# In-projection and gated recurrence as one program: heads' projections between the recurrence's tiles

## The chip, the cores and the metric

The kernel runs on one core of a Trainium2 chip. The metric is the device time of one execution in microseconds (us). TensorE (PE) multiplies, VectorE (DVE), ScalarE (ACT) and GpSimd (POOL) work elementwise, and SyncE (SP) issues most transfers. Each engine takes its instructions in program order; semaphores order the engines among each other.

## What is computed

Two layers over 1152 tokens: 1024 of a new stream (the prompt) and 8 running streams of 16 tokens (the sample). The change concerns the mixer of the first layer, from `hn = rmsnorm(x)`:

```python
z = hn @ w_in                                   # q, k: 4 heads x 128; v, g: 4 x 256; a: 16
la = log_sigmoid(a @ w_gate2 + b_gate) / 16     # per token, head and key channel
b  = cumsum(la)                                 # inside blocks of 64 (sample: 16) tokens
qd, kd = q * exp(b), k * exp(-b)
A  = tril(qd @ kd.T)
o  = qd @ s + A @ v                             # s: state of the head, 128 x 256
s  = s * exp(b_last) + (k * exp(b_last - b)).T @ v
o  = o / rms(o) * norm_g
h  = h + (o * silu(g)) @ w_out
```

After it come a SwiGLU, an attention layer on a shared K/V and a second SwiGLU, which the change leaves alone.

## The kernel before

Activations lie as 128 channels x tokens. The residual stream `S.res` (128 x 8 x 1152, 4.6 MB) stays in SBUF. A product of fp32 values is made of three PE products of rounded parts (`product`, lines 143 to 145: hi by hi, lo by hi, hi by lo). A weight unit of 512 KB is loaded to a stage, ACT casts its high part (L132), POOL subtracts to get the low part (L137), and only then may PE use it.

The first layer's mixer runs as three programs with a barrier between them.

1. **In-projection** (`project`, tag `in`). 25 units of 128 columns, each multiplied with three groups of 384 tokens (`GRP`): 8 x 3 products of 384 columns per group. `LateNorm` multiplies with the unnormalised stream: ACT rounds the operand (L400), DVE makes its low part (L412), then ACT squares the stream (L292), DVE adds the squares (L331 to L336), PE sums and spreads them (L313, L425), and ACT keeps the spread factor (L418), with which DVE scales each result (L574). Results go to DRAM (`gla_rows`). SP fetches the first four weight units and then issues `keep_strips` (L433): a 6 MB copy of the attention's bias rows to DRAM, read from 16 partitions, which nothing needs before the attention.
2. **Recurrence** (`gla_core`, tag `mix`). Head by head it reads q, k, v and g back. For each tile of 128 tokens PE makes the scores (L1525), the state update (L1531) and the output of the tile before it (L1494 scores by v, L1498 q by state); DVE masks the scores (L1763) and steps the state (L1778). The sample's eight streams are updated in turn (L1548, L1794). The next head's logits (L1453), decays (ACT Exp and Ln, L1569 to L1584, with ACT_TABLE_LOADs between; DVE scan, L1713) and transposes stand between the tiles.
3. **Out-projection** (`add_product`, tag `go`), which starts from `S.mixed` and `S.res`, both in SBUF.

The second layer's attention is built as the changed mixer will be: it projects its own q, k and v between its score tiles ("items" of 384 columns for q and k and of 256 for v), writes `S.res` to DRAM (`res_rows`) and uses its space. Its out-projection (`ao`) calls `add_product` with `reload=True`, which loads `S.mixed` (L600) and `S.res` (L609) from DRAM first.

Of the kernel before, what the change touches and what calls it, by code (L numbers as in the profile page):

```python
# [20 lines left out]
P = 128  # L21
# [33 lines left out]


class Segment:


    def __init__(self, w, col, units, gain, out, row, skip, base, slots):  # L60
        self.w, self.col, self.gain, self.out, self.row, self.skip = (
            w.rearrange("(k p) n -> p k n", p=P), col, gain, out, row, skip)
        self.per = min(slots, units)
        self.trips = units // self.per
        self.base, self.turn = base, base // slots
        assert base % slots == 0 and units % self.per == 0
# [367 lines left out]


def project(nc, S, tag, gain, segments, aside=None):


    SL, BANKS = 4, 6
    with semaphores(nc) as sem:  # L440
        filled = sem(f"{tag}_filled")
        drained = sem(f"{tag}_drained")
        stored = [sem(f"{tag}_stored{i}") for i in range(SL)]
        with ExitStack() as ctx:
            ring = weight_ring(nc, sem, ctx, tag, SL, SL)
            rows = ctx.enter_context(nc.sbuf_tensor(f"{tag}_sums", [P, SL, TOK], F32))
            ps = ctx.enter_context(nc.psum_tensor(f"{tag}_ps", [P, BANKS, 512], F32))
            nps = ctx.enter_context(nc.psum_tensor(f"{tag}_norm_ps", [P, 2, 512], F32))
            norm = LateNorm(nc, S, sem, ctx, f"{tag}_norm", gain, nps[:, 0, :], nps[:, 1, :GRP])
            block = ctx.enter_context(nc.Block())  # L450
            plan, base = [], 0
            for w, col, units, gain, out, row, skip in segments:
                plan.append(Segment(w, col, units, gain, out, row, skip, base, SL))
                base += units
            assert all(s.per == SL for s in plan[:-1])

            @block.sync
            def _(sp):
                def fetch(s, it, j):
                    fetch_unit(sp, ring, it * s.per + (s.base + j), j, s.w[:, :, bass.ds(it * (s.per * P) + (s.col + j * P), P)])  # L460

                def store(s, it, j):

                    sp.wait_ge(drained, it * (s.per * NG) + (BANKS + (s.base + j + 1) * NG))
                    sp.dma_start(s.out[bass.ds(it * (s.per * P) + (s.row + j * P), P - s.skip), :],
                                 rows[s.skip:, j, :]).then_inc(stored[j], 16)

                last = None
                for s in plan:
                    for j in range(s.per):  # L470
                        if last:
                            store(last, last.trips - 1, j)
                        fetch(s, 0, j)
                    if aside and s is plan[0]:
                        aside(sp, S)
                    if last:
                        for j in range(s.per, last.per):
                            store(last, last.trips - 1, j)
                    if s.trips > 1:
                        with sp.Fori(1, s.trips) as it:  # L480
                            for j in range(s.per):
                                store(s, it - 1, j)
                                fetch(s, it, j)
                    last = s
                for j in range(last.per):
                    store(last, last.trips - 1, j)
                for j in range(SL):
                    sp.wait_ge(stored[j], 16 * (1 + sum(s.trips for s in plan if j < s.per)))


            BEFORE = 2

            @block.scalar
            def _(act):
                def units(s, it, first, last):
                    for j in range(first, last):
                        unit = it * s.per + (s.base + j)
                        act.wait_ge(filled, (unit + 1) * NG)
                        round_unit(act, ring, unit, j, it + s.turn, s.gain)

                norm.round(act, 0)
                units(plan[0], 0, 0, BEFORE)
                for t in range(1, NG):
                    norm.round(act, t)
                norm.squares(act)
                units(plan[0], 0, BEFORE, SL)
                norm.root(act)
                norm.keep(act)
                for s in plan:
                    with act.Fori(1 if s is plan[0] else 0, s.trips) as it:  # L510
                        units(s, it, 0, s.per)

            @block.gpsimd
            def _(pool):
                def units(s, it, first, last):
                    for j in range(first, last):
                        unit = it * s.per + (s.base + j)
                        if s.gain is not None:
                            scale_unit(pool, ring, unit, j, it + s.turn, S.gains[:, s.gain, :])
                        split_unit(pool, ring, unit, j)  # L520

                pool.sem_inc(ring.split, SL)
                units(plan[0], 0, 0, SL)
                for s in plan:
                    with pool.Fori(1 if s is plan[0] else 0, s.trips) as it:
                        units(s, it, 0, s.per)

            @block.tensor
            def _(pe):
                def unit(s, it, j):  # L530
                    pe.wait_ge(ring.split, it * s.per + (s.base + j + 1 + SL))
                    for t in range(NG):
                        g = j * NG + t
                        if isinstance(it, int) and s is plan[0] and j == 0:
                            norm.ready(pe, t)

                        pe.wait_ge(drained, it * (s.per * NG) + (s.base * NG + g + 1))
                        for k in range(DK):
                            w, x = slice(k * P, (k + 1) * P), slice(t * GRP, (t + 1) * GRP)
                            m = product(pe, ps[:, g % BANKS, :GRP], ring.hi[:, j, w], ring.lo[:, j, w],  # L540
                                        S.x_hi[:, k, x], S.x_lo[:, k, x], k == 0, k == DK - 1)
                        m.then_inc(filled, 1)
                        if isinstance(it, int) and s is plan[0] and j == 1:

                            if t == 1:
                                norm.sum_all(pe)
                            if t == NG - 1:
                                norm.spread_all(pe)
# [2065 lines left out]
```

## Time and profile before

| | |
|---|---|
| median of 3 runs (range) | 3243.76 us (3236.13 to 3247.28) |
| profiled execution: its time, its span | 3243.13 us, 3241.4 us |
| mean granted TensorE clock | 0.933 |
| busy: PE, DVE, ACT, POOL | 91%, 40%, 28%, 31% |
| in-projection, first to last product | 35.1 to 368.9 us |
| first product of the out-projection `go` | 635.3 us |

The span goes from the first to the last instruction of the profiled execution. A granted clock of 1.0 is 2.4 GHz, 0.5 is 1.2 GHz. PE counts as busy while a product is in its pipeline.

### The profile page before, as it was taken

How to read it: one execution, taken by the hardware profiler on the slowest of the kernel's cores; microseconds unless marked ns; L12 is line 12 of the kernel's file. 1: busy time of each engine (PE TensorE's matmuls, PEld its weight loads, DVE VectorE, ACT ScalarE, POOL GpSimd, SP SyncE). 2: the span in 40 equal slices, each digit the busy share in tenths (PEclk: the TensorE clock that was granted, in tenths of full speed). 3: DMA queues.
4: the chain of work that ended last, by engine and by line, in shares of the span. 5: the costliest groups of instructions: out<-in, count | busy, mean ns of one | idle time of the engine just before them, and what ended most of it. 6: DMA issues, size and time to landing. Idle time of an engine off the chain costs nothing. (4 is left out here: it accounts for less than half of the span.)

```text
span 3241.4 us, 48505 instructions
## 1 busy us (share of the span) xinstructions
PE 2950.6 (91%) x19428; PEld 2791.7 (86%) x19428; DVE 1303.8 (40%) x2395; ACT 918.1 (28%) x1679; POOL 999.6 (31%) x655
## 2 busy tenths in 40 slices
PE   6899789796999999999889999994969999999997
PEld 6899667595999999999878887863959999999996
DVE  5111143516656555211323434343166555652114
ACT  3000244303322223210324434343033232332112
POOL 1221022314444345542221212101134444445420
PEclk9999776796999999999989999997969999999998
DMA  8523232302222223421312324336022222235211
GB/s 146 127 83 96 76 107 73 108 2 98 65 82 66 78 79 118 166 83 40 122 44 88 108 87 142 100 95 215 7 86 77 79 65 82 68 107 182 88 40 59
DMA packets 328252, 294.39 MB, mean 91 GB/s; under 512 B 23248, under 2 KB 306976, under 8 KB 327280
## 3 DMA queue, kind: packets, MB, share of 16 engines
q1 hardware_dynamic: 323168, 282.11, 28.8%
q10 hardware_dynamic: 4880, 9.44, 0.8%
q8 instruction: 142, 2.33, 0.3%
q14 instruction: 62, 0.51, 0.1%
HBM read 211.47 MB, written 95.76 MB: 95 GB/s over the span
## 5 line engine op out<-in xcount | busy, mean ns | idle before, releaser
L143 PE MATMUL f_ps<-f_x_hi,f_w_hi 128*128 128x288 f32 (+1 forms) x2976 | 932.1, 313 | 58.7 <-POOL f_x_lo L917 28.4
L144 PE MATMUL f_ps<-f_x_hi,f_w_lo 128*128 128x288 f32 (+1 forms) x2976 | 927.4, 312 | 0.0
L145 PE MATMUL f_ps<-f_x_lo,f_w_hi 128*128 128x288 f32 (+1 forms) x2976 | 925.1, 311 | 0.0
L143 PEld LDWEIGHTS f_ps<-f_x_hi,f_w_hi 128*128 128x128 f32 x2976 | 565.2, 190 | 65.9 <-issue 24.2
L145 PEld LDWEIGHTS f_ps<-f_x_lo,f_w_hi 128*128 128x128 f32 x2976 | 567.3, 191 | 0.0
L144 PEld LDWEIGHTS f_ps<-f_x_hi,f_w_lo 128*128 128x128 f32 x2976 | 566.4, 190 | 0.0
L904 POOL TENSOR_TENSOR f_w_lo<-f_w_whole,f_w_hi 128x512 fp32r<-128x512 f32 x136 | 188.7, 1396 | 391.8 <-DVE f_w_whole L1156 172.5
L1233 DVE TENSOR_TENSOR res<-res,f_ps 128x384 f32<-128x384 f32 x192 | 106.4, 554 | 457.7 <-PE f_ps L145 457.7
L1179 DVE TENSOR_TENSOR res<-f_ps,res 128x288 f32<-128x288 f32 x308 | 140.3, 458 | 209.2 <-PE f_ps L145 200.0
L143 PE MATMUL in_ps<-in_x_hi,in_w_hi 128*128 128x384 f32 x600 | 202.7, 338 | 21.8 <-POOL in_w_lo L137 20.2
L1179 DVE TENSOR_TENSOR f<-f_ps,f 128x288 f32<-128x288 f32 x308 | 139.9, 457 | 160.1 <-PE f_ps L145 149.8
L144 PE MATMUL in_ps<-in_x_hi,in_w_lo 128*128 128x384 f32 x600 | 202.1, 337 | 0.0
L145 PE MATMUL in_ps<-in_x_lo,in_w_hi 128*128 128x384 f32 x600 | 202.1, 337 | 0.0
L909 POOL TENSOR_TENSOR f_w_lo<-f_raw,f_w_hi 128x768 fp32r<-128x768 f32 (+1 forms) x64 | 109.2, 1706 | 268.3 <-ACT f_w_hi L1032 268.3
L143 PE MATMUL f_ps<-f_x_hi,spare 128*128 128x288 f32 x544 | 161.2, 296 | 1.3 <-DVE res L1179 1.3
L144 PE MATMUL f_ps<-f_x_hi,spare 128*128 128x288 f32 x544 | 160.5, 295 | 0.0
L145 PE MATMUL f_ps<-f_x_lo,spare 128*128 128x288 f32 x544 | 159.9, 294 | 0.0
L1032 ACT CAST f_w_hi<-f_raw 128x768 fp32r<-128x768 f32 (+1 forms) x64 | 50.1, 782 | 362.5 <-PE f_ps L145 354.1
L574 DVE TENSOR_TENSOR in_sums<-in_ps,in_norm_work 128x384 f32<-128x384 f32 x75 | 41.4, 557 | 264.5 <-PE in_ps L145 258.7
L137 POOL TENSOR_TENSOR in_w_lo<-in_stage,in_w_hi 128x1024 fp32r<-128x1024 f32 x25 | 60.0, 2404 | 261.3 <-ACT in_w_hi L132 261.3
L143 PEld LDWEIGHTS in_ps<-in_x_hi,in_w_hi 128*128 128x128 f32 x600 | 114.1, 190 | 22.9 <-issue 11.8
L922 POOL TENSOR_TENSOR f_x_lo<-f_x_whole,f_x_hi 128x1152 fp32r<-128x1152 f32 x44 | 118.3, 2695 | 37.7 <-ACT f_x_hi L1040 37.7
(283 smaller groups left out, 5619.1 us busy)
## 6 DMA issues: line engine op xcount, KB each, us to landing
f_x_whole<-hid_rows SPq DMA_DIRECT2D x44, 576.0 KB, 5.0
f_raw<-in_ffn_w_down SPq DMA_DIRECT2D x48, 384.0 KB, 3.4
gla_rows<-in_sums SPq DMA_DIRECT2D x24, 576.0 KB, 3.2
res_rows<-res SPq DMA_DIRECT2D x3, 4608.0 KB, 15.9
in_stage<-in_gla_w_in SPq DMA_DIRECT2D x25, 512.0 KB, 4.5
hid_rows<-f SPq DMA_DIRECT2D x44, 288.0 KB, 2.5
hid_rows<-res SPq DMA_DIRECT2D x44, 288.0 KB
f_raw<-in_ffn_w_gate SPq DMA_DIRECT2D x22, 512.0 KB, 3.9
```

The lines of the kernel that those rows point to most:

```text
L137: pool.tensor_tensor(r.lo[:, j % r.slots, :], r.stage[:, j % r.stages, :], f32(r.hi[:, j % r.slots, :]), ALU.subtract).then_inc(r.split, 1)
L143: pe.matmul(out, w_hi, x_hi, start=first, stop=False)
L144: pe.matmul(out, w_lo, x_hi, start=False, stop=False)
L145: return pe.matmul(out, w_hi, x_lo, start=False, stop=last)
L574: dve.tensor_tensor(rows[:, j, t * GRP:(t + 1) * GRP], ps[:, g % BANKS, :GRP], norm.work[:, t, :], ALU.mult).then_inc(drained, 1)
L904: pool.tensor_tensor(gu_weight(1, i, n), gu_sum(i, n) if name in SUMS else gu_raw(i, name), f32(gu_weight(0, i, n)), ALU.subtract).then_in ...
L909: pool.tensor_tensor(dn_weight(1, u), dn_raw(u), f32(dn_weight(0, u)), ALU.subtract).then_inc(w_split, 1)
L922: pool.tensor_tensor(h_lo[:, k % HS, :], h_sum[:, k % HS, :], f32(h_hi[:, k % HS, :]), ALU.subtract).then_inc(hid_split, 1)
L1032: act.copy(dn_weight(0, u), dn_raw(u)).then_inc(w_rounded, 1)
L1179: dve.tensor_tensor(sets[b][:, new, :], bank(i, n, b), sets[b][:, old, :], ALU.add).then_inc(made[b], 1)
L1233: dve.tensor_tensor(h, h, bank(u, t), ALU.add).then_inc(added, 1)
```

## The change

`project` and `gla_core` go; one program, `mixer`, takes their place. v and g are now made with the tokens as rows (items of 128 tokens x 256 columns, 24 products each), q and k in items of 384 tokens, the 16 gate columns `a` alone. Head 0's `a`, v, k and q come first (`BEGIN`). Then there are 36 slots (4 heads x 9 tiles). In a slot PE makes the scores and the state update, one whole item, the tile's output, and then the rest of the slot's items between small fills: `l` (logits of the next head), `k` (a transpose for the next tile) and `o` (transposes of the last head's gated output, three per slot in slots 0 to 2). `FILL_PLAN` says which items: this head's g in slots 0 to 2, the next head's k, q and v after; the last head has one g item a slot. v, gate, output, k and q lie in the space of `S.res`, which is written to DRAM before. Nothing passes through `gla_rows`. The output goes to `o_rows`, and `go` is called with `reload=True`.

```diff
-def project(nc, S, tag, gain, segments, aside=None):
...
-def gla_core(nc, S, a):
...
+def mixer(nc, S, a, tag):
...
+    FILL_PLAN = ("g0g1g2", "g3g4g5", "g6g7g8", "k0q0", "v0v1v2", "v3v4v5", "k1q1", "v6v7", "k2v8q2")
...
+    UNITS = [("a", 0, 0), ("v", 0, 0), ("v", 0, 1), ("k", 0, 0), ("q", 0, 0)]
...
+    LOGITS = {2: 0, 5: 1, 7: 2}
...
+                for x in UNITS[:ST]:
+                    fetch(x)
+                keep_strips(sp, S)
...
+                sp.dma_start(S.res_rows, S.res[:]).then_inc(spilled, 16)
+                for x in UNITS[ST:5]:
+                    fetch(x)
+                load_states(0)
...
+                        if t == 0:
+                            pe.wait_ge(w_split, UNIT[kind, h, 1 if kind in "vg" else 0] + 1)
+                        old = n - HELD if HELD <= n < HELD + 2 else n - 2 if n >= HELD else None
+                        if old is not None:
+                            pe.wait_ge(done[ITEMS[old][0]], COUNT[ITEMS[old]])
...
+                    if i < SAMPLE:
...
+                        pe.wait_ge(stepped, h * (NB + DEC_B) + 2 * i + 1)
+                        for c in range(0 if i else 1, 2):
+                            r = slice(c * BLK, (c + 1) * BLK)
+                            m = pe.matmul(dst[r], kq[:, 1, i * P + c * BLK:i * P + (c + 1) * BLK],
+                                          st[:, (2 * i + c) % STATES, :], start=False, stop=True,
+                                          tile_position=(0, c * BLK))
...
+                for x in BEGIN[:HELD]:
+                    piece(x, 0, DK)
+                norm.sum_all(pe)
+                norm.spread_all(pe)
+                for x in BEGIN[HELD:NG + NT]:
+                    piece(x, 0, DK)
+                for t in range(NG):
+                    pe.wait_ge(norm.kept, NG)
+                    fill(("l", t))
+                    for x in BEGIN[NG + NT + 2 * t:NG + NT + 2 * t + 2]:
+                        piece(x, 0, DK)
+                fill(("k", 0))
+                for s in range(SLOTS):
...
+                    scores(s)
+                    if i < SAMPLE:
+                        update(s)
+                    if run:
+                        piece(run[0], 0, 6 if i == SAMPLE else DK)
+                    out(s)
+                    if i == SAMPLE:
+                        for n in range(DEC_B):
+                            update_stream(h, n)
+                    if run and i == SAMPLE:
+                        piece(run[0], 6, DK)
+                    for n in range(max(len(run) - 1, len(fills))):
+                        if n < len(fills):
+                            fill(fills[n])
+                        if n + 1 < len(run):
+                            piece(run[n + 1], 0, DK)
...
+                def decays(n):
+
+                    is_taken(act, ("l", n))
+                    act.activation(ln[:], ln[:], ACT.Exp, scale=-1.0).then_inc(softplus, 1)
...
+                    act.activation(ln[:], ln[:], ACT.Ln, bias=1.0).then_inc(softplus, 1)
+                    act.wait_ge(decay, 3 * n + 3)
...
+                    act.activation(eb[:, 0, :], b_sum[:], ACT.Exp, scale=1.0 / GLA_TAU).then_inc(grown, 1)
+                    act.activation(eb[:, 1, :], b_sum[:], ACT.Exp, scale=-1.0 / GLA_TAU).then_inc(grown, 1)
...
+                norm.round(act, 0)
+                for x in UNITS[:1]:
+                    round_weights(x)
+                for t in range(1, NG):
+                    norm.round(act, t)
+                for x in UNITS[1:3]:
+                    round_weights(x)
+                norm.squares(act)
+                norm.root(act)
+                norm.keep(act)
+                act.wait_ge(norm.inverse, 1)
+                act.wait_ge(spilled, 16)
...
+                    if i == 0 and h:
+                        root(h - 1)
+                    for x in units_of(s):
+                        round_weights(x)
+                    square(s)
+                    for n in range(max(len(run), len(fills))):
...
+                            take(fills[n])
+                    for x in fills:
+                        if x[0] == "l":
+                            decays(x[1])
...
+                norm.split_all(dve)
+                norm.statistics(dve)
+                dve.wait_ge(norm.kept, NG)
+                dve.wait_ge(spilled, 16)
+                for t in range(NG):
+                    take_rank(t)
...
+                    mask(s)
+                    if i < SAMPLE:
+                        step(s)
...
+                    keep_out(s)
...
+                    for x in fills_of(s):
+                        if x[0] == "l":
+                            decays(x[1])
+                            scales(x[1])
...
-            with ExitStack() as phase:
-                operands(nc, S, phase, "in")
...
+            mixer(nc, S, a, "mix")
+        with nc.sbuf_tensor("gla_mixed", [P, DK, TOK], F32) as S.mixed:
+            add_product(nc, S, "go", a["gla_w_out"][0], reload=True)
```

`take` lets ACT read a fill from PSUM; `take_v`, `take_gate` (ACT, Silu) and `take_kq` (DVE) read the items. `take_rank` reads an `a` item. `scales` (DVE) multiplies the two exponentials of a third of the tokens with the norm's factor, and `take_kq` needs them.

## Rows read from the trace of the kernel before

**Rows 1.** Windows by stage: in-projection, recurrence, attention, 50 us of in-projection. Busy us (instructions), clock, DMA share, GB/s.
```profile
35.10:368.90 333.80, 321.42 (x1824) 319.03 (x1824) 64.82 (x116) 43.21 (x53) 57.58 (x24) 0.98 0.41 94
368.90:623.60 254.70, 206.06 (x1020) 157.66 (x1020) 107.98 (x201) 101.83 (x168) 64.49 (x60) 0.71 0.28 93
1650.00:2200.00 550.00, 518.48 (x4060) 435.35 (x4058) 206.76 (x599) 228.81 (x596) 88.70 (x79) 0.98 0.33 98
150.00:200.00 50.00, 50.00 (x290) 50.00 (x290) 6.69 (x12) 4.25 (x5) 9.58 (x4) 1.00 0.29 89
```

**Rows 2.** Timeline, SP, ACT and POOL: start us, us, what, idle before and releaser.
```profile
30.11 1.76 SPq L433 DMA_DIRECT2D strips<-bias_strip  x1
...
100.94 1.04 ACT L132 CAST in_w_hi<-in_stage 128x1024 fp32r<-128x1024 f32 x1 [31.99 <-DMA in_stage<-in_gla_w_in]
...
102.06 2.34 POOL L137 TENSOR_TENSOR in_w_lo<-in_stage,in_w_hi 128x1024 fp32r<-128x1024 f32 x1 [39.96 <-ACT in_w_hi L132]
```

**Rows 3.** Transfers by line: KB each, median us from issue to landing.
```profile
strips<-bias_strip SPq DMA_DIRECT2D x1, 6144.0 KB, 66.3
...
o_rows<-att_o SPq DMA_DIRECT2D x72, 64.0 KB, 2.3
```

**Rows 4.** The tile in_stage: its 25 loads.
```profile
DMA to landing us min/median/max: 4.0/4.5/29.3
```

**Rows 5.** Windows: end of the strips' copy; the attention writing S.res to DRAM.
```profile
95.00:100.00 5.00, 0.18 (x2) 0.00 (x0) 0.56 (x1) 0.00 (x0) 0.00 (x0) 0.83 1.03 338
...
1584.00:1588.00 4.00, 0.00 (x0) 0.00 (x0) 0.00 (x0) 1.04 (x1) 2.85 (x2) 0.50 1.02 442
```

**Rows 6.** Timeline, the in-projection's norm: first squares, last addition, last kept factor.
```profile
41.56 1.57 ACT L292 ACTIVATE in_norm_work<-res 128x768 f32<-128x768 f32 x2
...
56.98 0.56 DVE L336 TENSOR_TENSOR in_norm_acc<-in_norm_acc,in_norm_work 128x384 f32<-128x384 f32 x1
...
68.47 0.48 ACT L418 COPY in_norm_work<-in_norm_ps 128x384 f32<-128x384 f32 x1 [1.06 <-PE in_norm_ps L425]
```

**Rows 7.** Timeline, PE: first and last of an attention v item's 24 products.
```profile
1732.74 0.28 PE L143 MATMUL att_sums_ps<-att_wv_hi,att_x_hi 128*128 128x256 f32 x1
...
1735.49 0.28 PE L145 MATMUL att_sums_ps<-att_wv_lo,att_x_hi 128*128 128x256 f32 x1
```

**Rows 8.** Timeline, PE: fp32 products of the recurrence and of the attention.
```profile
595.07 0.44 PE L1525 MATMUL mix_score_ps<-mix_q,mix_k 128*128 128x128 f32 x2
595.43 0.70 PE L1531 MATMUL mix_update_ps<-mix_v,mix_k2t 64*128 64x256 f32 x4
596.07 0.49 PE L1494 MATMUL mix_out_ps<-mix_scores,mix_v 128*128 128x128 f32 x2
...
606.72 3.68 PE L1548 MATMUL mix_update_ps<-mix_v,mix_k_spread 128*128 128x256 f32 x12 [0.21 <-DVE mix_state_sample L1794]
...
2217.25 1.31 PE L2274 MATMUL att_turn_ps<-att_p_turned,res 128*64 128x128 f32 x20 [0.72 <-DVE att_p_turned L2521]
...
2220.53 0.65 PE L2286 MATMUL att_turn_ps<-att_v_cache,att_p_turned 128*32 128x128 f32 x16
```

**Rows 9.** Timeline, ACT and DVE: head 0's decays.
```profile
381.37 1.16 ACT L1569 ACTIVATE mix_soft<-mix_soft 128x1152 f32<-128x1152 f32 x1 [0.93 <-DVE mix_least L1705]
382.56 1.28 ACT L1571 ACT_TABLE_LOAD   x1
383.85 1.16 ACT L1571 ACTIVATE mix_soft<-mix_soft 128x1152 f32<-128x1152 f32 x1
...
388.91 2.56 DVE L1713 TENSOR_TENSOR_SCAN mix_b<-mix_reset,mix_least 128x1152 f32<-128x1152 f32 x1
```

**Rows 10.** Timeline: first product of go; end of the attention and first product of ao.
```profile
635.34 0.68 PE L143 MATMUL go_ps<-go_x_hi,go_w_hi 128*128 128x384 f32 x1 [17.06 <-POOL go_w_lo L137]
...
2223.05 0.53 ACT L2402 COPY att_o<-att_turn_ps 64x128 f32<-64x128 f32 x2 [0.55 <-PE att_turn_ps L2296]
...
2260.99 0.68 PE L143 MATMUL ao_ps<-ao_x_hi,ao_w_hi 128*128 128x384 f32 x1 [37.98 <-POOL ao_w_lo L137]
```

More of the change, by code:

```diff
@@ L54, in __init__ @@
         self.slots, self.stages = slots, stages
[L57 to L66, printed above, removed]
 class Shared:
@@ L433, in keep_strips @@
     sp.dma_start(S.strips, S.strip[:].unsqueeze(1).to_broadcast([HEADS, P, STRIP])).then_inc(S.strips_kept, 16)
-def project(nc, S, tag, gain, segments, aside=None):
[L439 to L548, printed above, removed]
-                pe.sem_inc(filled, SL * NG)
-                for j in range(SL):
-                    unit(plan[0], 0, j)
-                for s in plan:
-                    with pe.Fori(1 if s is plan[0] else 0, s.trips) as it:
-                        for j in range(s.per):
-                            unit(s, it, j)
-            @block.vector
-            def _(dve):
-                dve.sem_inc(drained, BANKS)
-                for j in range(SL):
-                    dve.sem_inc(stored[j], 16)
-                norm.split_all(dve)
-                norm.statistics(dve)
-                dve.wait_ge(norm.kept, NG)
-                for s in plan:
-                    with dve.Fori(0, s.trips) as it:
-                        for j in range(s.per):
-                            dve.wait_ge(stored[j], (it + s.turn + 1) * 16)
-                            for t in range(NG):
-                                g = j * NG + t
-                                dve.wait_ge(filled, it * (s.per * NG) + (SL * NG + s.base * NG + g + 1))
-                                dve.tensor_tensor(rows[:, j, t * GRP:(t + 1) * GRP], ps[:, g % BANKS, :GRP],
-                                                  norm.work[:, t, :], ALU.mult).then_inc(drained, 1)
@@ new lines, in sums_bank, with turn_bank, is_taken, weights @@
+            def sums_bank(x):
+                n = PLACE[x]
+                place = (gps[:, 0], gps[:, 1], sps[:], ops[:], ups[:, 0], ups[:, 1])[n] if n < HELD else gps[:, n % 2]
+                return place[:RANK if x[0] == "a" else P, :width(x)]
+            def turn_bank(x):
+                return tps[:, FILL[x] % 2, :]
+            def is_taken(engine, x):
+                engine.wait_ge(taken[FILL[x] % 2], FILL[x] // 2 + 1)
+            def weights(x):
+                kind, _, half = x
+                if kind in "vg":
+                    return wv_hi[:, half, :], wv_lo[:, half, :]
+                n = (DK * RANK) if kind == "a" else D
+                slot = 1 if kind == "q" else 0
+                return w_hi[:, slot, :n], w_lo[:, slot, :n]
@@ L1575, in take_v @@
-                def take_v(h, b, n):
-                    at = prep(h, "v", n)
-                    w = min(2, NT - 2 * n)
-                    act.copy(v[:, b, 2 * n:2 * n + w, :].rearrange("p i d -> p (i d)"),
-                             is_filled(at)[:, :w * GLA_DV]).then_inc(taken[at[0]], 1)
-                def grow(h, b):
-                    act.wait_ge(decay, h * 3 + 3)
-                    act.activation(eb[:, b, :], b_sum[:], ACT.Exp, scale=1.0 / GLA_TAU).then_inc(grown, 1)
-                    act.activation(least[:], b_sum[:], ACT.Exp, scale=-1.0 / GLA_TAU).then_inc(grown, 1)
@@ L1802, in attention @@
+                for i in range(NT):
+                    gate_out((H - 1) * NT + i)
 def attention(nc, S, a, tag):
```

952 lines of the change are left out of this document (533 added, 419 removed).

## The prediction

> **What bounds the kernel now.** I read the windows by stage first. In the in-projection PE is the bound: busy in 321 of 334 us at a granted clock of 0.98. The recurrence after it also keeps PE busy for 206 of 255 us, but at a clock of 0.71: waits and short products leave it near the lower of its two levels much of the time [rows 1]. The attention, built as the new mixer will be, has projection items between its small products; it is granted 0.98 and PE is idle in 31.5 of 550 us [rows 1]. So there is something to win: the recurrence's PE work at nearly full clock, with its waits covered by items. Then I read the timeline at the start and the transfers, because the new program issues its loads in another order, and last the seams between programs. `go` makes its first product at 635.3 us [rows 10]; behind it nothing is changed. So the sum is the new time of that product.
>
> **The prologue (the largest cost).** SP fetches only two units, the gate columns and half of head 0's v weights, before it issues the 6 MB copy of the strips. Behind that come the 4.7 MB write of `S.res` and only then the second half of the v weights, without which no v item may start. That copy needs 66.3 us [rows 3] after 30.1 [rows 2], so it is out at 96.4. A weight unit issued behind it in the old kernel landed after 29.3 us instead of the usual 4.5 [rows 4]: ACT had it at 100.9 after 32 us of waiting, and POOL had been idle 40 us [rows 2]. In the five microseconds after the copy the queue moved 338 GB/s [rows 5]. One queue serves these in order. Four units stood ahead of the copy, now little more than one, so it ends some 4.5 us sooner (1.5 MB at 338 GB/s): 92. `S.res` at 442 GB/s [rows 5] takes 10.7 us: 103. The unit's own 4.5 us [rows 4] and three small tables between (1.5 us, my estimate, a third of a unit's landing): 109, bounds 104 to 114. ACT's cast of 1.0 and POOL's 2.3 us [rows 2] put the first v item at 112.5. The three `a` items need 12 us from about 35, and no faster than their operands come; so PE stands for some 60 us.
>
> It gets worse because ACT takes its work in order: the cast that waits for this unit stands ahead of the squares of the norm. What is queued behind it is the whole statistics chain. In the old kernel that ran from 41.6 to 57.5 [rows 6] beside products; I take 14 of these 16 us, as DVE was still making low parts in the first of them: from 110 to 124. From the last addition to the last kept factor it took 57.5 to 69.0, 11.4 us [rows 6]: 135.4. Only then may DVE take `a` item 0 (0.6 us, rows 6's addition is as wide) and PE begin its seventh item: 136. Six v items of 24 products at 0.1196 us (2.75 us between the first and the last start [rows 7]) are 2.87 us each, 17.2 together; 1.5 more for a low clock after the pause: 154.8.
>
> Then three rounds of logits, k and q. A q or k item is 24 x 50/290 = 4.14 us [rows 1], a logits product 0.7. The next round's k item waits until its predecessor's sums are taken, and these need the decays. That chain from the logits, in thirds of the old kernel's width: two reads by ACT 1.0; Exp and Ln, each 1.28 for the table and 0.5 (a 384-wide copy is 0.48 [rows 6, 9]), 3.6; DVE 0.56 and a third of the scan's 2.56, 1.4; two exponentials 1.0; scaling 1.3; eight handovers near 0.1: about 9. It ties with PE's own 9.0 a round: three rounds make 27. The first slot starts at **182** (bounds 165 to 195).
>
> **The slots.** Items: 36 of g and 27 of v at 2.87 (180.8) and 18 of k and q at 4.14 (74.5): 255. Recurrence, at full clock: a score 0.36 and a state update 0.64 [rows 8]. Score by v is new in its shape: between 0.32 (half of the two updates) and 0.61 (a sixth of the stream's row [rows 8]), taken at 0.45. The two products by state go to two halves of PE's columns: 0.52 if they overlap as the attention's do (20 records of half the width in 1.31), 0.9 if not; taken at 0.62, nearer the row of the same kind. With a transpose of 0.2 a tile takes 2.27; 32 of them 72.6. A sample tile: 0.36, 0.45, eight products into quarters of the columns (1.3 by the attention's row, 3.6 without overlap; two in turn share a quarter, so 2.8), a fill 0.2, eight stream updates at the old pace of 0.61: 8.7, four times 34.8. Nine logits at 0.7 and 27 output fills at 0.3: 14.4. Together 122, bounds 108 to 138. Items and recurrence: **377**.
>
> **Waits in the slots.** DVE's mask and two steps of a tile, narrower than rows 6's addition of 0.56, need under 1.7 us and are covered by the item of 2.87; without an item they would be a wait of that size in each of 32 tiles. Two things are not.
> First the decays. On DVE `decays` and `scales` stand ahead of the next tile's mask, and on ACT behind the evictions of the slot. From the logits fill to that mask, the chain of 9 us with a copy and the mask at its end, it takes 9.7 us where ACT is free, but PE has only a fill, a score, an update and a k item in between, 5.3: 4.4 us, twice (slot 2 of heads 1 and 2). In slot 5, and slot 2 of head 0, ACT first takes two more items, 6.4 + 8.4 against 11.2 of cover: 3.6, four times. In slot 7 it is 3.5 + 8.4 against 6.5, since the sample tile has only six eighths of a k item ahead of its output: 5.4, three times. Sum 39.
> Second the gate weights. They take the place of v's, so they are cast after a head's last v item: eviction 0.5 (as the copy of rows 6), a table and the root 1.6, a cast 1.0 and two subtractions of 2.34 make 7.8; PE has a q item, a score and an update, 5.1. 2.7 us three times, 4.7 for head 0: 13. Waits together **52**, bounds 15 (the attention's idle share of 5.7% would be 21) and 85. POOL's other work and SP's loads (states, k and q weights) have a slot or more to spare.
>
> Clock: by the attention's 0.98 [rows 1] 377 becomes 385, **8** more; bound, at the recurrence's 0.71 for its 122 us, 47 more than that.
>
> **The end.** Nine outputs go through a ring of three buffers: three landings of 2.3 [rows 3] and nine evictions of 0.5 after the root: **11**. Then `go` reloads what it had in SBUF. From the attention's last ACT copy to the first product of `ao` took 37.9 us, `S.res` and the outputs coming in: **38** (the old seam had 17 us of idle PE [rows 10]).
>
> Sum: 182 + 377 + 52 + 8 + 11 + 38 = 668, against 635.3: 32 us more. The profiled execution took 3243.1 us, its span 3241.4, 0.6 below the median of the runs. I predict **3275**. Without the prologue's pause the same change would be a gain of some fifty: the program starts its slots 85 us later than the products before them need (63 us from 34).
>
> The function tables are where the Trainium skill (ScalarE: Activation LUTs, What ACT_TABLE_LOAD costs) speaks more strongly against this change: it counts a drain of 1.38 us beside each load of 1.28. This case's trace shows the load's 1.28 and no drain: the activation before ends at 382.53, the load runs from 382.56, the next begins at 383.85 [rows 9]. By the page the twelve decay chains, with two loads each, would cost 33 us more, 3308.
>
> **Rivals.** *Clock falls* (0.12): the waits of 3 to 5 us in every third slot bring the old recurrence's 0.71 back for its products; 47 more, 3322. For it speaks that stage's clock, against it the attention, whose tiles are as small. *Waits are hidden* (0.18): the chains at the end of slots 2, 5 and 7 are shorter than my thirds or PE's small products slower, so that items cover them. At most 52 less, 3223; it is faster from 42 on, so at least four fifths must vanish. The attention's 5.7% of idle speaks for half of it. *The queue does not hold* (0.13): the second half of v lands beside the copy, as other loads do in 4.5 us. Then v and the statistics run at once, but `S.res` must still be out at 104 before any sum may be taken, so item seven starts at 105 instead of 136: 31 less, 3244, no change. The 29.3 us speak against it. *A table change holds ACT twice as long* (0.02): 24 loads in the chains at 1.28 more, 31, 3306; the 0.01 us between load and activation speak against it.
>
> **Chances.** Forecast 0.55, and the rivals as given. Slower by over 0.3% (10 us, about what a measurement of this kernel can tell from no change): 0.55 + 0.12 + 0.02 = 0.69; no change 0.13; faster 0.18. The forecast's own range is 3252 to 3300; to hold 8 in 10 I go from 3226, where the waits almost vanish, to 3318, short of the fallen clock.
>
> **What would show it.** Right: PE without work for some 60 us until 112, DVE's first take of an `a` item near 136, slot 0's first score near 182; pauses of 3 to 5 us ahead of the products by v in slots 3, 6 and 8 with DVE's mask as releaser, and ahead of the first g item with POOL; a clock near 0.97 in the slots; some 38 us without products ahead of `go`. Wrong: v's second half landing before 60, a clock under 0.9 in the slots, a mask that is never last, or slots that last under 400 or over 480 us in all (437 by the sum).

## The result, and the profile after

The changed kernel takes 3298.1 us (median of four runs, 3294.3 to 3301.0) against 3240.9 for the kernel before: ratio 1.0174, 95% interval 1.0152 to 1.0197. It is slower, as forecast, by 57 us instead of the 32 of the sum. Its profiled execution took 3294.3 us.

The windows answer to [rows 1]: prologue, slots and seam up to the first product of `go`, then slots 3 and 4 of head 0. Columns as there.

```profile
26.00:176.50 150.50, 79.24 (x464) 66.67 (x465) 41.78 (x81) 52.39 (x81) 11.22 (x7) 0.73 0.56 102
176.50:643.00 466.50, 400.36 (x2581) 335.18 (x2579) 123.50 (x274) 149.47 (x331) 74.97 (x95) 0.93 0.15 43
643.00:691.00 48.00, 5.75 (x18) 2.64 (x18) 14.41 (x13) 19.46 (x27) 4.48 (x1) 0.52 0.85 290
217.78:237.46 19.68, 14.25 (x64) 12.00 (x63) 4.67 (x10) 8.97 (x13) 5.87 (x5) 0.74 0.18 54
237.46:248.40 10.94, 10.94 (x87) 9.77 (x86) 2.15 (x5) 1.50 (x5) 0.40 (x1) 1.00 0.00 0
```

Slot 4 is what the change is meant to be: PE has no gap and the full clock. Slot 3 has 23 products fewer and takes nearly twice as long: PE is idle for 5.4 us and its clock is 0.74 in the mean, between the two levels 0.5 and 1.0 (1.2 and 2.4 GHz).

The view of waits for PE (us in total, times, longest), its longest rows of the mixer and the seam alone, says where most of the mixer's idle time is:

```profile
PE mix_out_ps L131 <- POOL mix_wv_lo L1396: 60.4, 1, 60.4
PE go_ps L131 <- POOL go_w_lo L125: 38.7, 1, 38.7
PE mix_sums_ps L131 <- POOL mix_wv_lo L1396: 13.6, 4, 5.0
PE mix_out_ps L1540 <- DVE mix_scores L1786: 13.2, 6, 3.0
PE mix_update_ps L1523 <- ACT mix_k2t L1652: 11.1, 13, 1.1
PE mix_out_ps L1552 <- DVE mix_scores L1786: 10.8, 3, 3.6
PE mix_sums_ps L131 <- POOL mix_w_lo L1396: 8.8, 1, 8.8
PE mix_turn_ps L1494 <- POOL mix_k L1407: 8.5, 3, 3.4
PE mix_turn_ps L1499 <- ACT mix_mixed L1658: 6.8, 7, 2.9
...
```

The first is the pause in the prologue, the second the seam, the seventh the start, where the first weights (those of `a`) must be split. The rest lies in the slots: gate weights (third), mask (fourth and sixth), and three that the prediction did not have (fifth, eighth and ninth; of the ninth's 6.8 us 5.8 lie in the slots, the rest behind the last one).

The strips' copy and what stood behind it (transfers by line; timeline of SP, ACT and PE) answer to [rows 2] and [rows 3]:

```profile
strips<-bias_strip SPq DMA_DIRECT2D x1, 6144.0 KB, 64.1
```

```profile
27.32 0.69 SPq L421 DMA_DIRECT2D strips<-bias_strip  x1
...
104.66 1.04 ACT L1603 CAST mix_wv_hi<-mix_w_stage 128x1024 fp32r<-128x1024 f32 x1 [63.69 <-DMA mix_w_stage<-in_gla_w_in]
...
108.28 0.55 PE L131 MATMUL mix_out_ps<-mix_wv_hi,mix_x_hi 128*128 128x256 f32 x1 [60.41 <-POOL mix_wv_lo L1396]
...
128.97 0.55 PE L131 MATMUL mix_sums_ps<-mix_wv_hi,mix_x_hi 128*128 128x256 f32 x1 [1.24 <-DVE mix_squares L1725]
...
691.23 0.68 PE L131 MATMUL go_ps<-go_x_hi,go_w_hi 128*128 128x384 f32 x1 [38.65 <-POOL go_w_lo L125]
```

The second half of the v weights is cast at 104.7, PE starts on it at 108.3, the seventh projection item ("item seven", the first that needs a PSUM bank emptied by DVE) at 129.0, slot 0 at 176.5, and `go` at 691.2, 55.9 later than in [rows 10]. Behind `go` the profiled execution is 4.7 us shorter than before (3294.3 - 691.2 against 3243.1 - 635.3). Over the profiles of this study the part from `go` to the end of the span took 2594.8 to 2610.9 us, so one profile can't place 5 us there.

### The profile page after: what moved, and what is told of

It is laid out like the page before. It is cut to its first block and busy times, and to the rows that moved or that the text cites. A ratio compares the mean times of both kernels' runs of the same rounds, so it can differ in the third digit from the quotient of the medians.

```text
span 3292.2 us, 49193 instructions
## 1 busy us (share of the span) xinstructions
PE 2904.7 (88%) x19644; PEld 2717.3 (83%) x19644; DVE 1292.5 (39%) x2436; ACT 972.3 (30%) x1875; POOL 960.8 (29%) x672
## 5 line engine op out<-in xcount | busy, mean ns | idle before, releaser
L131 PEld LDWEIGHTS f_ps<-f_x_hi,f_w_hi 128*128 128x128 f32 x2976 | 564.1, 190 | 68.1 <-issue 25.6
L131 PE MATMUL mix_sums_ps<-mix_wv_hi,mix_x_hi 128*128 128x256 f32 x552 | 166.7, 302 | 14.8 <-POOL mix_wv_lo L1396 13.6
L132 PE MATMUL mix_sums_ps<-mix_wv_hi,mix_x_lo 128*128 128x256 f32 x552 | 160.6, 291 | 0.0
L133 PE MATMUL mix_sums_ps<-mix_wv_lo,mix_x_hi 128*128 128x256 f32 x552 | 160.5, 291 | 0.0
L131 PEld LDWEIGHTS mix_sums_ps<-mix_wv_hi,mix_x_hi 128*128 128x128 f32 x552 | 110.5, 200 | 29.7 <-POOL mix_wv_lo L1396 15.2
L131 PE MATMUL att_sums_ps<-att_x_hi,att_w_hi 128*128 128x384 f32 x352 | 128.0, 364 | 0.0
L873 ACT CAST f_w_hi<-f_w_whole 128x512 fp32r<-128x512 f32 x136 | 84.4, 622 | 140.0 <-DVE f_w_whole L999 68.3
```

Source lines behind the costliest of these rows:

```text
L131: pe.matmul(out, w_hi, x_hi, start=first, stop=False)
L132: pe.matmul(out, w_lo, x_hi, start=False, stop=False)
L133: return pe.matmul(out, w_hi, x_lo, start=False, stop=last)
L873: act.copy(gu_weight(0, i, n), gu_sum(i, n) if name in SUMS else gu_raw(i, name)).then_inc(w_rounded, 1)
```

## The experiments

Times are medians; the ratio is to the kernel before, timed on the same chip. "Less" and "more" are against the changed kernel's 3298.1 where nothing else is named. Theory and rival are those of the expectation.

### The prologue

**The second half of v ahead of the copy.**

```diff
-                for x in UNITS[:ST]:
+                for x in UNITS[:3]:
                     fetch(x)
                 keep_strips(sp, S)
...
-                for x in UNITS[ST:5]:
+                for x in UNITS[3:5]:
                     fetch(x)
```

> The second half of head 0's v weights is issued ahead of the strips' copy; the write of the stream stays behind it. Queue theory (one queue serves its transfers in order, and the copy holds up first the v weights and then the write of S.res): the first v item follows the a items near 48 us, the statistics end near 70, but no sum may be taken before S.res is out near 103, so the seventh item starts near 104 instead of 129.0: 25 us less, 3273. Rival (only ACT's order, the squares behind the cast, costs anything, and the write of S.res is hidden): the seventh item starts near 70, 59 us less, 3239.

Measured: 3284.9, ratio 1.0127 (1.0110 to 1.0144), 13 less, half of the 25 of the queue theory (the profile has 17 at `go`, 674.6 instead of 691.2). The wait for v is gone, and another stands in its place (view of waits; then the tile `res_rows`, whose write was issued at 68.1):

```profile
PE mix_sums_ps L131 <- DVE mix_squares L1725: 45.3, 1, 45.3
```

```profile
DMA to landing us min/median/max: 42.1/42.1/42.1
```

PE's item seven needs a bank that DVE may empty only once `S.res` has been written, and that write landed at 68.1 + 42.1 = 110.2; DVE's first take began at 110.3, PE at 110.9 instead of 129.0. The theory had the write out at 103. Two things stood behind the copy, and the wait for v hid the wait for the write.

**The copy out of the prologue**, into slot 4 of head 0, with the fetches as in the last run:

```diff
-                keep_strips(sp, S)
...
                     for x in units_of(s):
                         fetch(x)
+                    if s == 4:
+                        sp.wait_ge(s_filled, s)
+                        keep_strips(sp, S)
```

> Now the copy of the strips is issued in slot 4 of head 0, and all of the prologue's transfers stand ahead of it. Queue theory: S.res is out near 45 us, the statistics end near 70 as they did in the old kernel, the seventh item starts near 70 and slot 0 near 117 instead of 176.5: 59 us less, 3239, the time of the kernel before. Rival (the copy holds up later loads instead, the gate weights of head 1 above all): part of it comes back as a wait in head 1's slot 0, 3260 or more.

Measured: 3236.3, ratio 0.9980 (0.9969 to 0.9992): 62 less, as both numbers of the trace have it (slot 0 at 114.1 instead of 176.5, `go` at 628.8 instead of 691.2). The windows are the prologue and the slots:

```profile
26.00:114.14 88.14, 76.78 (x464) 64.70 (x465) 43.27 (x81) 52.30 (x81) 11.61 (x7) 0.88 0.32 103
114.14:580.80 466.66, 400.30 (x2581) 335.16 (x2579) 123.48 (x274) 149.68 (x331) 75.07 (x95) 0.93 0.27 57
```

The waits in the slots are those of the changed kernel to 0.1 us. So the copy's place cost 62 us, together with the order of the loads behind it: what the place gives with v's second half still behind the write was not run. At its new place (issued at 155.8) the copy is as slow as before, 64.0 us, and two weight units issued behind it landed after 41.2 and 55.8 us; but nothing needs them sooner, and the trace shows no cost.

**The same early copy on another queue.**

```diff
-                keep_strips(sp, S)
...
+                keep_strips(act, S)
                 norm.round(act, 0)
```

> The changed kernel with the strips' copy issued at the same early time, but on ACT's queue instead of SP's. Theory (the pause is an order on one queue): the v weights and the written copy of the activations land beside it, the first slot starts between 114 and 122 us, 3236 to 3246. Rival (the copy holds the DMA engines, whatever queue it is on): loads beside it stay slow, PE still waits 20 us or more for v, 3260 or more.

Measured: 3297.7, ratio 1.0162 (1.0147 to 1.0177). Nothing is gained, so the order on one queue, the theory of the prediction, is not what makes the pause. The views are the waits, the tile `res_rows` (the write was issued at 36.2 on SP's queue, ahead of v's second half), ACT's casts of the two halves of v, and two windows:

```profile
PE mix_out_ps L131 <- POOL mix_wv_lo L1395: 59.3, 1, 59.3
```

```profile
DMA to landing us min/median/max: 65.0/65.0/65.0
```

```profile
50.64 1.04 ACT L1602 CAST mix_wv_hi<-mix_w_stage 128x1024 fp32r<-128x1024 f32 x1 [10.31 <-DMA mix_w_stage<-in_gla_w_in]
104.01 1.04 ACT L1602 CAST mix_wv_hi<-mix_w_stage 128x1024 fp32r<-128x1024 f32 x1 [52.33 <-DMA mix_w_stage<-in_gla_w_in]
```

```profile
40.00:60.00 20.00, 8.35 (x49) 4.34 (x46) 1.59 (x3) 1.37 (x2) 2.34 (x1) 0.80 0.99 119
60.00:80.00 20.00, 0.00 (x0) 0.00 (x0) 0.00 (x0) 0.00 (x0) 0.00 (x0) 0.50 0.96 102
```

With SP's queue free of the copy, the write of `S.res` took 65.0 us, where the median of the four such writes of this kernel is 16.6. The share of the DMA engines is 0.96 to 0.99 while they move 102 to 119 GB/s: the copy holds the engines, not only a queue. v's first half, with only the small unit of `a` ahead of it on SP's queue, is cast at 50.6 instead of 39.9. Its second half still stood behind the write on SP's queue, so this run does not say what the copy alone would have cost it; the kernel before, below, shows a unit that waits without such a write. The Trainium skill says of the engines (DMA: Bandwidth & Descriptors, Issuing engines are not separate DMA queues) that transfers started by different engines run on the same 16 DMA engines and interleave there. By that rule a second queue frees nothing, and the trace agrees (3297.7 against 3298.1 us).

**The copy from DRAM.** The 16 rows go to DRAM once (48 KB, 3.9 us), and from there into the other 127 places of each:

```diff
-    sp.dma_start(S.strips, S.strip[:].unsqueeze(1).to_broadcast([HEADS, P, STRIP])).then_inc(S.strips_kept, 16)
+    sp.dma_start(S.strips[:, 0, :], S.strip[:]).then_inc(S.strips_kept, 16)
+    sp.wait_ge(S.strips_kept, 16)
+    sp.dma_start(S.strips[:, 1:, :], S.strips[:, 0, :].unsqueeze(1).to_broadcast([HEADS, P - 1, STRIP])
+                 ).then_inc(S.strips_kept, 16)
...
```

> The changed kernel, the strips' copy at its old place, but in two steps: the 16 rows once to DRAM, and from there to the other 127 copies of each. The copy from SBUF reads 16 partitions and keeps the DMA engines busy at 0.94 to 1.0 while it moves 102 GB/s. Theory (the read from 16 partitions is what is slow): a copy from DRAM to DRAM took 5.9 us for 960 KB in this kernel, 163 GB/s, so 6 MB take some 38 us instead of 64: 20 to 30 us less, 3268 to 3278. Rival (it is the rows of some 3 KB that are written, wherever they come from): within 6 us of 3298.

Measured: 3266.8, ratio 1.0082 (1.0056 to 1.0108), 31 less, just beyond the theory's 20 to 30. Transfers by line, waits, and the window of the copy:

```profile
strips<-strips SPq DMA_DIRECT2D x1, 6096.0 KB, 27.9
```

```profile
PE mix_out_ps L131 <- POOL mix_wv_lo L1399: 28.8, 1, 28.8
```

```profile
32.00:60.00 28.00, 13.98 (x72) 7.21 (x72) 9.64 (x18) 9.31 (x19) 3.47 (x2) 0.74 0.84 264
```

Rows of the same length, written to the same places but for one in 128, take less than half the time: it is the read from SBUF that is slow, not the write. That it is slow because it reads only 16 partitions is likely, as the write of `S.res` reads 128 and moves 442 GB/s [rows 5]; no run changed the number of partitions alone. The Trainium skill has a rule for it (SBUF — State Buffer, Door 1: The DMA port swizzle): a transfer's bandwidth depends on how many of SBUF's 16 DMA ports its partitions reach; partitions 0 to 15 reach four, and it gives 104 GB/s for 1 MiB. The window from 60 to 80 us of the last run, 102 GB/s, agrees.

**The kernel before with its copy on ACT's queue** (issued at the start of the in-projection instead of behind four weight units), and **with the copy from DRAM** at its old place. The edits are those of the last two runs, made in the kernel before.

> The kernel before, with the same copy issued on ACT's queue at the start of the in-projection. Theory (there the copy was hidden but for one wait of PE of 10.9 us for a low part): 0 to 11 us less than before, 3232 to 3243. Rival (the old order lost as much to the copy as the new one): some 60 us less, 3180.

> The kernel before with the same two-step copy of the strips, at its place behind four weight units. Its in-projection waits 20.2 us (two waits, the longer 10.9) for POOL's low parts while the slow copy runs. Theory (these two waits are what the old order paid for the copy, the new one paid 60): the copy ends 35 us sooner and 10 to 20 us of them go, 3222 to 3232. Rival (the old order hid the copy whole, the two waits come from somewhere else): within 6 us of 3242.

Measured: 3265.0, ratio 1.0063 (1.0050 to 1.0076); and 3229.3, ratio 0.9957 (0.9940 to 0.9974). The first missed: I had expected a small gain from a free queue, and the copy now ran beside the first weight units: ACT waited 31.2 us for the second, with the high parts of `x` behind it, and PE 29.6 for low parts that DVE makes of them:

```profile
64.53 1.04 ACT L132 CAST in_w_hi<-in_stage 128x1024 fp32r<-128x1024 f32 x1 [31.19 <-DMA in_stage<-in_gla_w_in]
```

```profile
PE in_ps L143 <- DVE in_x_lo L412: 29.6, 1, 29.6
```

Only the first unit stood ahead of this one on SP's queue, and the copy was on ACT's: this wait is the engines'. The second run hit in its time. PE's waits for POOL in the old in-projection, in the kernel before and with the copy from DRAM:

```profile
PE in_ps L143 <- POOL in_w_lo L137: 20.2, 2, 10.9
```

```profile
PE in_ps L143 <- POOL in_w_lo L137: 10.9, 1, 10.9
```

The wait that is left is that for the program's first weights, at 35 us in both, which I had counted to the copy; the other, 9.3 us, was the copy's. So the old order too paid for the copy, some 13 us; that the four units ahead of it were cover for the rest fits the first run, which lost 23 us without this cover.

### The slots

**The next keys ahead of the v weights on POOL.**

```diff
+                    if s + 1 < SLOTS:
+                        make_k2(s + 1)
                     for x in units_of(s):
                         split_unit_(x)
-                    if s + 1 < SLOTS:
-                        make_k2(s + 1)
```

> On POOL the next tile's scaled keys are made ahead of the slot's weight subtractions, not behind them. Theory: in slot 3 PE waited 2.4, 2.8 and 3.4 us for POOL's keys because two subtractions of 2.4 us stood ahead of them; that goes, and with it part of the low clock behind it: 9 to 15 us less, 3283 to 3289. Rival: the subtractions are then late for the v items of slot 4, and the wait only moves there: no change.

Measured: 3286.2, ratio 1.0135 (1.0118 to 1.0152), 12 less, as the theory had it; the wait for `mix_k` is gone from the list. In the changed kernel POOL's row in slot 3 reads

```profile
225.69 4.76 POOL L1396 TENSOR_TENSOR mix_wv_lo<-mix_w_stage,mix_wv_hi 128x1024 fp32r<-128x1024 f32 x2 [15.29 <-ACT mix_wv_hi L1603]
230.42 0.75 POOL L1407 TENSOR_TENSOR mix_k<-res,mix_eb_last 128x128 f32<-128x128 f32 x2
```

POOL had been idle for 15.3 us waiting for ACT's cast, with a key of 0.4 us behind it that PE needed.

**The mask ahead of the decays on DVE.**

```diff
                     mask(s)
                     if i < SAMPLE:
                         step(s)
+                    if s:
+                        for x in fills_of(s - 1):
+                            if x[0] == "l":
+                                decays(x[1])
+                                scales(x[1])
...
-                    for x in fills_of(s):
-                        if x[0] == "l":
-                            decays(x[1])
-                            scales(x[1])
```

> On DVE the decays and scales of a slot's logits are moved behind the next tile's mask and state steps. Theory: the waits for the mask in slots 3, 6 and 8 (13.2 and 10.8 us in nine places) go, and the low clock that followed those of slot 3: 24 to 36 us less, 3262 to 3274. Rival: the chain of decays is late for the next k item's sums instead, PE waits there for a free bank, and little is won: 3290 or more.

Measured: 3284.2, ratio 1.0128 (1.0105 to 1.0151), 14 less, between theory and rival. The mask waits are gone, all 24 us. What moved, and the window of all slots:

```profile
PE mix_turn_ps L1494 <- POOL mix_k L1407: 19.3, 3, 6.7
...
PE mix_update_ps L1530 <- DVE mix_state_sample L1817: 7.9, 11, 2.0
```

```profile
176.52:627.50 450.98, 390.85 (x2581) 333.97 (x2579) 123.35 (x274) 149.30 (x331) 75.88 (x95) 0.94 0.15 45
```

10.8 us come back at the keys, since slot 3 only waits longer at its next step, and 7.2 at the sample tile's state steps (0.7 before), now behind the decays on DVE. PE's idle time in the slots fell by 6 us only (466.5 - 400.4 = 66.1 to 451.0 - 390.9 = 60.1), its busy time by 9.5, with the same 2581 products at a mean granted clock of 0.94 instead of 0.93.

**All three repairs.**

> The strips' copy in slot 4, the keys ahead of the v weights on POOL, and the mask ahead of the decays on DVE, all three. Theory (three separate causes): against the copy alone (3236) the mask waits of 24 us and the key waits of 8.5 us go, some 7 us of waits on DVE's state steps come, and the clock in the slots rises a little: 3204 to 3214, the first product of the next program near 600. Rival (the waits only change their name, as 10.8 of 24 us did when the mask alone was moved): 3218 to 3230.

Measured: 3201.3, ratio 0.9867 (0.9853 to 0.9882), 97 less than the changed kernel and 40 less than the one before, 3 beyond the theory. Windows: all slots, then slot 3 of head 0.

```profile
114.93:546.50 431.57, 389.78 (x2581) 331.54 (x2579) 123.50 (x274) 148.77 (x331) 75.33 (x94) 0.95 0.29 61
156.49:167.17 10.68, 10.68 (x64) 9.51 (x63) 5.05 (x11) 8.77 (x13) 2.76 (x2) 1.00 0.79 87
```

Slot 3 shrinks from 19.7 to 10.7 us: 5.4 were waits, 3.6 the clock (PE busy for 14.25 us, and for 10.68 with the same 64 products). Over the slots idle time falls by 24 us and busy time by 10.6. Key and mask orders are worth 35 us together (3236.3 to 3201.3), against 12 and 14 alone: slot 3 of the first three heads waits for both, and with one mended the other still holds it (14.4 to 16.9 us with the keys first, 19.1 to 19.7 with the mask first, 10.7 to 13.1 with both).

**The output right behind scores and state update, the item after it.**

```diff
+                    out(s)
                     if run:
                         piece(run[0], 0, 6 if i == SAMPLE else DK)
-                    out(s)
```

> The changed kernel with a tile's output issued right behind its scores and its state update, the item after it. Theory (the item between them is the cover that makes the new order work): mask and state steps are now waited for in each of 32 tiles, 1.1 to 1.7 us each, and the three mask waits a head grow: 35 to 65 us more than 3298, so 3333 to 3363. Rival (PE's queue covers that anyway, the place of the item does not matter): within 10 us of 3298.

Measured: 3314.4, ratio 1.0222 (1.0207 to 1.0237): 16 more, neither number. Slot 4 of head 0 took 11.06 us instead of 10.94. Its timeline, PE and DVE:

```profile
236.71 0.38 PE L1511 MATMUL mix_score_ps<-res 128*128 128x128 f32 x2
237.02 0.70 PE L1523 MATMUL mix_update_ps<-res,mix_k2t 64*128 64x256 f32 x4
237.73 0.70 PE L1540 MATMUL mix_out_ps<-res,mix_scores 128*128 128x256 f32 x2
238.36 0.65 PE L1548 MATMUL mix_out_ps<-mix_state,res 128*64 128x256 f32 x4
...
237.38 0.29 DVE L1786 COPY_PREDICATED mix_scores<-causal,mix_score_ps 128x128 f32<-128x128 int32 x1
237.77 1.06 DVE L1809 SCALAR_TENSOR_TENSOR mix_state<-mix_state,mix_eb_last,mix_update_ps 128x256 f32<-128x256 f32 x2
```

PE goes from one product to the next without a wait: the state update of 0.70 us covers the mask, and the two products by v (L1540) cover the first state step, all that the products by state (L1548) wait for. The item pays off only where the decay chain stands ahead of the mask (slots 3, 6 and 8):

```profile
PE mix_out_ps L1540 <- DVE mix_scores L1786: 39.3, 6, 7.4
PE mix_out_ps L1552 <- DVE mix_scores L1786: 20.6, 4, 6.7
```

That is 59.9 against 24.0. Part of it is given back: the keys' wait is gone, gate weights cost 8.9 instead of 13.6, and the last head's slots 4 to 7 take 5.72 us instead of 6.37, as ACT's eviction of the next keys comes sooner.

### The seam

**Another order of the reloads**, on top of the three repairs, in `go` and `ao`:

```diff
+                fetch_unit(sp, ring, 0, 0, wv[:, :, 0:P])
                 if reload:
                     for t in range(NG):
...
-                if reload:
-                    act.dma_start(S.res[:], S.res_rows).then_inc(res_in, 16)
...
+                round_first(0)
                 for t in range(NG):
...
                     act.copy(S.x_hi[:, :, cols], S.mixed[:, :, cols]).then_inc(rounded, 1)
+                    if reload and t == 0:
+                        act.dma_start(S.res[:], S.res_rows).then_inc(res_in, 16)
...
```

`round_first(j)` is ACT's rounding of unit j of the first four, moved out of its loop.

> The three repairs together (3201), and in both products that reload their operands (go and ao) another order: the first weight unit is fetched ahead of the reload of the mixer's output, ACT rounds it first, and the reload of the activations is issued only when the first third of the output has landed. Theory (the 38.9 us ahead of each are an order of transfers and of ACT's work): 15 to 20 us less at each seam, 3160 to 3172. Rival (the reload is bound by the bytes, 11 MB at some 290 GB/s, whatever their order): 3195 or more.

Measured: 3185.6, ratio 0.9826 (0.9806 to 0.9847): 16 less than with the three repairs for both seams, half of the theory. PE:

```profile
PE go_ps L131 <- DVE go_x_lo L506: 29.2, 2, 18.9
```

The first product comes 20 us sooner (18.9 of waiting instead of 38.9), but after two thirds of the first unit (48 products) it waits 10.3 again for the last third of the output, which now shares the engines with `S.res` and the weights. From 575.0 to 595.3 the DMA share is 0.99 at 339 GB/s. So order was worth half of what the theory had; that the bytes are the other half fits this share, but no run shows it.

**The last head's prompt tiles with the output ahead of the item**, on top of that (`out(s)` moved as above, but only for `h == H - 1 and i < SAMPLE`).

> All the repairs and the other reload order, and in the last head's prompt tiles the output ahead of the item. The slots of the last head there were 5.72 us long with the output first and 6.37 with the item first, as ACT's eviction of the keys comes in time. Theory: 0.65 less in five slots and some 2 in each of three: 4 to 9 us less than the kernel with the item first. Rival (the same within 2 us, since the gain is taken back by the low clock after the waits).

Measured: 3170.6, ratio 0.9785 (0.9765 to 0.9806): 15 less than with the item first, more than the 4 to 9 of the theory. The head's first eight slots went from 68.5 to 57.2 us (slot 0 alone from 13.9 to 10.6), 11 of the 15; the rest is within what one profile leaves open. PE's waits for ACT's keys and outputs fell by 6.4 of these 11 (11.4 + 6.8 to 8.5 + 3.3). This is the fastest version: 70 us below the kernel before, 128 below the changed one.

## Why the prediction was right on the sign and short on the size

**By the sum.** `go` was put at 668 and came at 691.2, 23 late, as the time was (3298 against 3275).

| term | predicted | measured |
|---|---|---|
| first slot | 182 | 176.5 |
| slots: PE busy | 377 + 8 = 385 | 400.4 |
| slots: waits | 52 | 66.1 |
| end and reload | 49 | 48.2 |

**The prologue was right in number and too narrow in its reason.** PE paused 60.4 us (60 forecast) and item seven came at 129 (136). But "One queue serves these in order" does not make the pause: the copy on its own queue made the same one, in the kernel before ACT waited 31.2 us for a unit on the other queue, and the copy from DRAM halved the pause. The cause is a slow copy that keeps the DMA engines busy; the order on SP's queue, which put v's second half behind the write in the changed kernel and in that run alike, adds to it, by how much no run shows. The rival *the queue does not hold* failed too: its time needed loads that land beside the copy as fast as alone. Its other half was right, that `S.res` would be the next to hold item seven (predicted at 105; at 110.9 with v first). One reading is off without weight: the 338 GB/s of [rows 5] hold from 95 to 100 us, of which the first 1.4 still belong to the copy by the prediction's own 96.4; it moves the sum by some 1 us.

**The slots were mis-sized by 29.5 us**, from 25 us of waits that it did not price, 15 of busy time and some 4 of small differences, less 15 for the mask that it priced too high (the two errors in the waits cancel in part, which is luck):
- The gate weights cost 13.6 (13 forecast), the mask 24 (39): the decay chain was three fifths as late as worked out.
- "POOL's other work and SP's loads (states, k and q weights) have a slot or more to spare" is the step that failed. POOL takes in order, and in slot 3 two v units that wait for ACT stand ahead of the next keys: 8.5 us. ACT's evictions were not priced as releasers either: 11.1 for the keys' transposes in 13 tiles and 5.8 for the outputs. 25 us together.
- Clock: "8" was taken from the attention's 0.98; the slots had 0.93, with 0.74 in slot 3. Where no wait stands, the prices hold: slot 4 took 10.94 us against 3 x 2.87 + 2.27 = 10.9. The 15 us of extra busy time belong to slots with waits in part: repairs that took 24 us of idle time took 10.6 of it with them. The rest stays open. The rival *clock falls* was right in kind, with at most a third of its 47 us. *Waits are hidden* was not: 66.1 us are left.

**The cover was misjudged.** "Without an item they would be a wait of that size in each of 32 tiles" is wrong: a plain tile lost 0.12 us. The item between scores and output covers part of the decay chain in slots 3, 6 and 8 of the first three heads, worth 16 us in all.

**"A gain of some fifty" without the pause** was too much: 62 us came back, not 85, and left the kernel 0.2% below the one before. Two things fell short: the slots had lost 29 more than forecast, and without the pause the first slot came at 114.1, not at the 97 of "63 us from 34" (PE was busy for 76.8 us up to it, at a mean granted clock of 0.88). With the key and mask orders mended, the program is 40 us faster.

**Tables.** *A table change holds ACT twice as long* did not happen. Behind slot 2 of head 0 an activation ends at 217.98 + 0.47 = 218.45, the load follows at 218.47 and the next activation at 219.77:

```profile
217.98 0.47 ACT L1618 ACTIVATE res<-mix_sums_ps,mix_norm_rms 128x256 f32<-128x256 f32 x1 [2.35 <-PE mix_sums_ps L133]
218.47 1.28 ACT L1667 ACT_TABLE_LOAD   x1
219.77 0.53 ACT L1667 ACTIVATE mix_ln<-mix_ln 128x384 f32<-128x384 f32 x1
```

The drain of 1.38 us beside each load that the Trainium skill counts (ScalarE: Activation LUTs, What ACT_TABLE_LOAD costs) does not show here either. The decay chains made 28 loads and not the 24 of the prediction: the first of each head loads for its first Exp too.

## What to carry to other kernels

Price a merged program by what each engine's next instruction waits for, all engines alike: here the engines take work in order, and much of the missed waiting stood behind an instruction that was itself waiting (a key of 0.4 us behind two weight splits). Two causes that meet in one slot show their worth only together: 12 and 14 us alone, 35 both. Before a transfer is called hidden, look at its GB/s beside its DMA share: here a share near 1 at 100 GB/s was a copy that held up every load measured beside it, on whatever queue: a second queue did not help, another place or another source did. When one wait is taken away, ask what stood behind the same cause; taking away 60 us of waiting for v gained 13, and 24 of waiting for masks 14.

## What the runs showed that was not expected

- A copy of 6 MB that reads 16 partitions of SBUF held the DMA engines at a share of 0.94 to 0.96 with 102 to 103 GB/s (windows of the changed kernel from 40 to 90 us) and took 64 us, and a write of 4.6 MB on another queue took 65.0 us beside it (median of the four such writes 16.6). The same rows read from DRAM took 27.9 us.
- Two waits of 3.05 and 2.39 us in a slot of 20 us came with a granted clock of 0.74 and cost 3.6 us of slower products on top of their 5.4.
- The best place for the projection item was not the same in all heads: ahead of the output while decays are made in between, behind it in the last head (15 us).
